# A hybrid decoder layer on one core: the last block of FFN down products computed with tokens on the partitions, the second layer norm taken along the rows

## The chip, the cores and the metric

One NeuronCore of a Trainium2 chip runs the whole layer as one program. The metric is device time of one execution in microseconds (us). The engines are named as in the profile: PE is TensorE (PEld its weight loads), DVE VectorE, ACT ScalarE, POOL GpSimd, SP SyncE, which here only issues DMAs.

## The reference, cut to what matters

The layer handles 1024 prompt tokens and 32 sample tokens (8 sequences of 4), 1056 in all, of 1024 features. After attention, the state space branch and a first norm, the part that matters is:

```python
def swiglu_ffn(h, w_ffn_gate, w_ffn_up, w_ffn_down):
    g = jnp.einsum('btd,df->btf', h, w_ffn_gate)
    u = jnp.einsum('btd,df->btf', h, w_ffn_up)
    return jnp.einsum('btf,fd->btd', jax.nn.silu(g) * u, w_ffn_down)
...
    h = layer_norm(ALPHA * x + mix, ln1_g, ln1_b)
    y = layer_norm(ALPHA * h + swiglu_ffn(h, w_ffn_gate, w_ffn_up, w_ffn_down), ln2_g, ln2_b)
```

`D_FF` is 2816, everything is float32. `y` (1056 x 1024) goes to HBM with one token per row.

## The kernel before

Activations stand transposed, features on the 128 partitions and the 1056 tokens along the free dimension: `mm[P, KT, TOK]` is the residual, KT = 8 feature tiles. Products of near float32 precision are made of three products of rounded halves (`whi`/`wlo` for weights, `ahi`/`alo` or `fhi`/`flo` for activations: hi·hi, hi·lo, lo·hi). SP loads each weight unit (128 x 1024) into `raw`; POOL splits it into `whi` (L771) and then `wlo` (L773) in one of two slots, and starts a unit only when PE is done with the one that had its slot (`unit_done`); `unit_split` tells PE that both halves are there.

The FFN runs over NF = 11 blocks of 256 hidden features. In each, gate and up products (`dense`) are followed by `down` of the block before: two weight units, in each four feature tiles, the tile of 1056 tokens in three PSUM banks; DVE adds every result into `mm` (L2674). The blocks of the loop leave the last block's down products over, and the stage after the loop does these together with the norm.

That stage (the ending) goes by thirds of CH = 352 tokens. PE's `last_down(c, e0, e1)` makes for third c and feature tile e one PSUM bank in six products of 352 columns (L1642). DVE's `last_down` adds the bank into `mm` (L2870) and keeps a running sum over the tiles in `srow` (L2875). `mean` multiplies `srow` by a matrix of ones (L1567), ACT writes the mean row (L2051), DVE subtracts it (`centre`, L2775), ACT squares (L2058), DVE adds the squares of the eight tiles (`add_squares`, L2782), PE sums them over the partitions (L1574), ACT takes the root (L2063), DVE the reciprocal (L2787), PE spreads it over the partitions (`spread`, L1582), ACT copies it to `rsrow` (L2068), DVE multiplies by it and the gain (`scale`, L2790) and ACT adds the bias (`biased`, L2113). Then `by_token(i)` turns each tile of 128 tokens by eight transposes (L1659), ACT and DVE each copy half of it into `ytok[i]` (L2118, L2886), and SP stores it (L754). There are nine such tiles, the last with the 32 sample tokens (NS). The order on each engine is the order in which the code is written; waits are on semaphores counted, and a table `taken` gives second names to old semaphores (`step` is DVE's own, which it awaits before it reads what its last instruction wrote).

Of the kernel before, what the change touches and what calls it, by code (L numbers as in the profile page):

```python
# [11 lines left out]
ALU = mybir.AluOpType  # L12
# [3 lines left out]
P = 128  # L16
# [81 lines left out]
TS = 88  # L98
# [49 lines left out]
def build(nc, a, o, stop=99, debug=None):  # L148
# [6 lines left out]
             "tok_turned": ("x_turned", 9), "g_hi": ("x_hi", 9), "g_split": ("x_split", 9),  # L155
             "affine_ready": ("keys_turned", 9), "scaled": ("keys_out", 9), "centred": ("crow_turned", 6),
# [12 lines left out]
             "part_done": ("pre_ready", 36), "part_read": ("cb_read", 36), "squares_added": ("bf_ready", 2), "left_read": ("bt_read", 36), "uk_turned": ("norm_rooted", 2), "uk_ready": ("norm_inverted", 2), "lat_ready": ("norm_row", 6),  # L169
             "qlat_ready": ("norm_read", 6), "right_read": ("prod_ready", 32)}  # L170
# [239 lines left out]
    for pp in range(2):  # L410
# [3 lines left out]
        if pp == 1:  # L414
# [25 lines left out]
    stat, inv = ar("stat", [P, TOK // TS]), ar("inv", [P, TOK // TS])  # L440
    part, gnorm = ar("part", [P, TOK]), [rsrow, ar("gnorm1", [P, TOK])]
    ar = Arena(low)
    fhi, flo = ar("fhi", [P, 4, TOK], F32R), ar("flo", [P, 4, TOK], F32R)
    sq4 = [sq2[:, 0], sq2[:, 1], srow[:, :], murow[:, :]]
# [3 lines left out]
    sqb = [yz[:, :, :].rearrange("p a n -> p (a n)")[:, 0:KT * CH].rearrange("p (e n) -> p e n", n=CH),  # L448
           Arena(low + 34048 + 9 * 4096)("sqb", [P, KT, CH])]
# [24 lines left out]
    def _(sp):  # L474
# [425 lines left out]
    def _(pe):  # L900
# [668 lines left out]
        def square_sums(c, n):  # L1569

            pe.wait_ge(sem("row_read"), k["row_read"].held())
            pe.wait_ge(sem("squares_added"), k["squares_added"].next())
            for t in range(CH // TS):
                last = pe.matmul(ps[0:TS, 7, CH + t:CH + t + 1], sqb[n][:, 0, t * TS:(t + 1) * TS], ones[:, 0:1], start=True, stop=True)  # L1574
            last.then_inc(sem("sums_done"), k["sums_done"].adds(1))
# [16 lines left out]
        square_sums(0, 0)  # L1592
# [3 lines left out]
        square_sums(1, 0)  # L1596
# [3 lines left out]
        square_sums(2, 0)  # L1600
# [28 lines left out]
        for b in range(2):  # L1629
            pe.wait_ge(sem(f"res_free{b}"), k[f"res_free{b}"].next())  # L1630

        def last_down(c, e0, e1):

            for e in range(e0, e1):
                if c == 0 and e % 4 == 0:
                    pe.wait_ge(sem("unit_split"), k["unit_split"].next())
                if c * KT + e >= 6:
                    pe.wait_ge(sem("part_read"), k["part_read"].next())
                for i in range(6):
                    j, part = divmod(i, 3)  # L1640
                    w, x = ((whi, fhi), (whi, flo), (wlo, fhi))[part]
                    last = pe.matmul(ps[:, (c * KT + e) % 6, 0:CH], w[e // 4][:, j * 512 + e % 4 * P:j * 512 + (e % 4 + 1) * P], x[:, j, third(c)],  # L1642
                                     start=i == 0, stop=i == 5)
                last.then_inc(sem("part_done"), k["part_done"].adds(1))

        thirds_scaled = [0]

        def by_token(i):
            n = P if i < 8 else NS
            if i == 0:  # L1650
                pe.wait_ge(sem("part_read"), k["part_read"].next(6))
            if i >= 3:
                pe.wait_ge(sem("left_read"), k["left_read"].next())
                pe.wait_ge(sem("right_read"), k["right_read"].next())
            while thirds_scaled[0] * CH < i * P + n:
                pe.wait_ge(sem("affine_ready"), k["affine_ready"].next(KT))
                thirds_scaled[0] += 1
            for e in range(KT):
                last = pe.transpose(ps[0:n, 2 * (i % 3) + e // 4, e % 4 * P:(e % 4 + 1) * P], mm[:, e, i * P:i * P + n], ident)  # L1659
            last.then_inc(sem("tok_turned"), k["tok_turned"].adds(1))  # L1660

        last_down(0, 0, 8)
        last_down(1, 0, 3)
        mean(0)
        last_down(1, 3, 8)
        last_down(2, 0, 2)
        mean(1)
        square_sums(0, 1)
        last_down(2, 2, 6)
        spread(0)  # L1670
        last_down(2, 6, 8)
        mean(2)
        square_sums(1, 1)
        by_token(0)
        by_token(1)
        spread(1)
        square_sums(2, 1)
        spread(2)
        for i in range(2, 9):
            by_token(i)  # L1680
# [4 lines left out]
    def _(act):  # L1685
# [367 lines left out]
        def squares(c, n):  # L2053
            for h in range(2):
# [3 lines left out]
                act.activation(sqb[n][:, 4 * h:4 * h + 4, :], mm[:, 4 * h:4 * h + 4, third(c)], ACT.Square).then_inc(sem("squared"), k["squared"].adds(1))  # L2058
# [17 lines left out]
        squares(0, 0)  # L2076
        mean_row(1)
        root_of(0)
        squares(1, 0)
# [4 lines left out]
        squares(2, 0)  # L2084
# [25 lines left out]
        def biased(c):  # L2110
            for e in range(KT):
                act.wait_ge(sem("scaled"), k["scaled"].next())
                act.activation(mm[:, e, third(c)], mm[:, e, third(c)], ACT.Identity, bias=vecs[:, V_L2B + e:V_L2B + e + 1]).then_inc(sem("affine_ready"), k["affine_ready"].adds(1))  # L2113

        def left_half(i):
            n = P if i < 8 else NS
            act.wait_ge(sem("tok_turned"), k["tok_turned"].next())
            act.activation(ytok[i][0:n, 0:512], ps[0:n, 2 * (i % 3), :], ACT.Copy).then_inc(sem("left_read"), k["left_read"].adds(1))  # L2118

        mean_row(0)  # L2120
        squares(0, 1)
        mean_row(1)
        root_of(0)
        squares(1, 1)
        factor_row(0)
        mean_row(2)
        biased(0)
        root_of(1)
        squares(2, 1)
        factor_row(1)  # L2130
        left_half(0)
        left_half(1)
        biased(1)
        root_of(2)
        factor_row(2)
        left_half(2)
        biased(2)
        for i in range(3, 9):
            left_half(i)
# [3 lines left out]
    def _(dve):  # L2143
# [633 lines left out]
        def add_squares(n):  # L2777

            for h in (4, 2, 1):
                dve.wait_ge(sem("squared") if h == 4 else step.sem, k["squared"].next(2) if h == 4 else step.same())  # L2780
                total = k["squares_added"] if h == 1 else step
                dve.tensor_tensor(sqb[n][:, 0:h, :], sqb[n][:, 0:h, :], sqb[n][:, h:2 * h, :], ALU.add).then_inc(total.sem, total.adds(1))  # L2782
# [24 lines left out]
        add_squares(0)  # L2807
# [3 lines left out]
        add_squares(0)  # L2811
# [5 lines left out]
        add_squares(0)  # L2817
# [47 lines left out]
        def last_down(c, e0, e1):  # L2865

            at = third(c)
            for e in range(e0, e1):
                dve.wait_ge(sem("part_done"), k["part_done"].next())
                dve.tensor_tensor(mm[:, e, at], ps[:, (c * KT + e) % 6, 0:CH], mm[:, e, at], ALU.add).then_inc(sem("part_read"), k["part_read"].adds(1))  # L2870
                if e:
                    dve.wait_ge(sem("part_read"), k["part_read"].same())
                    dve.wait_ge(step.sem, step.same())
                    total = k["srow_ready"] if e == KT - 1 else step
                    dve.tensor_tensor(srow[:, at], mm[:, 0, at] if e == 1 else srow[:, at], mm[:, e, at], ALU.add).then_inc(total.sem, total.adds(1))  # L2875

        def scale_third(c):
            dve.wait_ge(sem("row_read"), k["row_read"].next())
            dve.wait_ge(sem("centred"), k["centred"].same())
            for e in range(KT):  # L2880
                scale(e, V_L2G, c)

        def right_half(i):
            n = P if i < 8 else NS
            dve.wait_ge(sem("tok_turned"), k["tok_turned"].next())
            dve.tensor_copy(ytok[i][0:n, 512:1024], ps[0:n, 2 * (i % 3) + 1, :]).then_inc(sem("right_read"), k["right_read"].adds(1))  # L2886

        last_down(0, 0, 8)
        last_down(1, 0, 3)
        centre(0)  # L2890
        last_down(1, 3, 8)
        add_squares(1)
        last_down(2, 0, 2)
        centre(1)
        inverse(0)
        last_down(2, 2, 8)
        add_squares(1)
        scale_third(0)
        centre(2)
        inverse(1)  # L2900
        add_squares(1)
        right_half(0)
        right_half(1)
        scale_third(1)
        inverse(2)
        right_half(2)
        scale_third(2)
# [25 lines left out]
```

## Time and profile before

| | |
|---|---|
| median of 3 timed runs | 2940.25 us (2938.14 to 2943.52) |
| profiled execution, its own time | 2930.37 us |
| its span in the trace | 2928.3 us |
| busy: PE, PEld, DVE, ACT, POOL | 96%, 86%, 51%, 26%, 35% |
| mean granted TensorE clock | 0.978 of full speed |

The span is what the trace shows from the first to the last instruction; the profiled execution took 2.1 us more. Times below count from the start of the span. The granted clock is given in parts of full speed: 1.00 is 2.4 GHz and 0.50 is 1.2 GHz. Neighbouring matmuls overlap in the trace, so what one costs in a stream is the distance of the starts and not its duration.

### The profile page before, as it was taken

The numbers are of one execution on the slowest core, as the hardware profiler recorded it, in microseconds if no ns is written. First come the engines' busy times: TensorE is split into PE (matmuls) and PEld (weight loads), VectorE is DVE, ScalarE is ACT, GpSimd is POOL, SyncE is SP. The second block draws the span as 40 slices with busy tenths as digits, with TensorE's granted clock in tenths as the row PEclk, the third lists the DMA queues.
The fourth block names the chain that finished last, engine by engine and source line by source line (L and its number), as shares of the span: only waits on it lengthen the run. The fifth ranks groups of instructions, "written<-read, shape, count | busy, mean of one in ns | idle before, by whom it ended". The sixth has DMA issues, their size and how long they took to land.

```text
span 2928.3 us, 45789 instructions
## 1 busy us (share of the span) xinstructions
PE 2821.5 (96%) x18912; PEld 2529.6 (86%) x18912; DVE 1501.4 (51%) x2094; ACT 762.3 (26%) x1193; POOL 1015.2 (35%) x603
## 2 busy tenths in 40 slices
PE   8999999999999999999999799999899999999996
PEld 7999999899999984555666599999799999999995
DVE  3535777766665655555344457863732222222227
ACT  2112112444454534454332321100310000000004
POOL 3443333333333315444112033444143333333330
PEclk9999999999999988999999899999999999999998
DMA  4363233565656644222534243343111111111101
GB/s 142 83 205 100 81 110 107 168 168 163 173 156 167 155 143 111 60 59 66 198 136 191 90 142 125 133 149 108 37 44 51 43 43 50 43 43 44 49 21 60
DMA packets 314482, 308.68 MB, mean 105 GB/s; under 512 B 32069, under 2 KB 272970, under 8 KB 311850
## 3 DMA queue, kind: packets, MB, share of 16 engines
q1 hardware_dynamic: 252104, 194.97, 23.6%
q10 hardware_dynamic: 58650, 73.89, 7.4%
q0 software_dynamic: 3584, 37.75, 3.4%
q8 instruction: 108, 1.77, 0.2%
q14 instruction: 36, 0.29, 0.0%
HBM read 228.36 MB, written 78.20 MB: 105 GB/s over the span
## 4 chain that ended last, share of the span: by engine, by line
PE 79%; DVE 11%; ACT 4%; issue 3%; DMA 1%; POOL 1%; ACTq 0%; SPq 0%; DVEq 0%; POOLq 0%
PE ps L964 41%; PE ps L1145 12%; PE ps L1279 4%; DVE cv L2287 3%; PE ps L1303 2%; PE ps L1293 2%; PE ps L1437 2%; PE ps L1413 2%; PE ps L1393 2%; PE ps L1178 1%; PE ps L1182 1%; PE ps L1171 1%; DVE cv L2281 1%; DVE cv L2289 1%; PE ps L1224 1%
## 5 line engine op out<-in xcount | busy, mean ns | idle before, releaser
L771 POOL TENSOR_TENSOR whi<-raw,cst 128x1024 fp32r<-128x1024 f32 x160 | 312.5, 1953 | 1151.2 <-PE ps L964 946.7
L773 POOL TENSOR_TENSOR wlo<-raw,whi 128x1024 fp32r<-128x1024 f32 x160 | 432.0, 2700 | 12.6
L964 PE MATMUL ps<-ahi,whi 128*128 128x352 f32 x1728 | 375.7, 325 | 2.1 <-POOL wlo L773 1.4
L964 PE MATMUL ps<-alo,whi 128*128 128x352 f32 x1728 | 375.6, 325 | 0.0
L964 PE MATMUL ps<-ahi,wlo 128*128 128x352 f32 x1728 | 372.4, 324 | 0.0
L964 PEld LDWEIGHTS ps<-ahi,whi 128*128 128x128 f32 x1728 | 294.7, 189 | 2.7 <-POOL wlo L773 1.7
L964 PEld LDWEIGHTS ps<-ahi,wlo 128*128 128x128 f32 x1728 | 296.8, 189 | 0.0
L964 PEld LDWEIGHTS ps<-alo,whi 128*128 128x128 f32 x1728 | 295.4, 188 | 0.0
L1145 PE MATMUL ps<-xhi,whi 128*128 128x352 f32 x768 | 255.9, 333 | 0.5 <-ACT xraw L1775 0.5
L1145 PE MATMUL ps<-xhi,wlo 128*128 128x352 f32 x768 | 247.8, 323 | 0.0
L1145 PE MATMUL ps<-xlo,whi 128*128 128x352 f32 x768 | 247.7, 323 | 0.0
L877 POOL TENSOR_TENSOR pr<-pr,rowinv 128x384 f32<-128x384 f32 (+7 forms) x128 | 145.6, 1146 | 192.0 <-DVE rowinv L2493 191.8
L2488 DVE TENSOR_REDUCE negmax<-ps 128x1 f32<-128x384 f32 (+7 forms) x128 | 97.0, 758 | 140.0 <-PE ps L1281 139.3
L1279 PE MATMUL ps<-kb,qb 96*128 96x512 f32 (+3 forms) x384 | 161.3, 539 | 6.0 <-ACT pr L1903 2.7
L2674 DVE TENSOR_TENSOR mm<-ps,mm 128x1056 f32<-128x1056 f32 x80 | 100.6, 1257 | 116.3 <-PE ps L964 116.3
L964 PE MATMUL ps<-xhi,whi 128*128 128x352 f32 x672 | 147.9, 329 | 5.2 <-ACT xraw L1775 3.9
L1279 PEld LDWEIGHTS ps<-kb,qb 96*128 96x128 f32 x384 | 65.6, 198 | 100.3 <-issue 84.5
L1145 PEld LDWEIGHTS ps<-xhi,whi 128*128 128x128 f32 x768 | 144.3, 188 | 8.7 <-issue 6.2
L964 PE MATMUL ps<-xlo,whi 128*128 128x352 f32 x672 | 147.2, 327 | 0.0
L964 PE MATMUL ps<-xhi,wlo 128*128 128x352 f32 x672 | 145.9, 326 | 0.0
L1145 PEld LDWEIGHTS ps<-xlo,whi 128*128 128x128 f32 x768 | 144.4, 188 | 0.0
L1145 PEld LDWEIGHTS ps<-xhi,wlo 128*128 128x128 f32 x768 | 144.3, 188 | 0.0
(372 smaller groups left out, 5082.3 us busy)
## 6 DMA issues: line engine op xcount, KB each, us to landing
raw<-in_w_in SPq DMA_DIRECT2D x61, 512.0 KB, 5.0
s_a<-d_acum SPq DMA_DIRECT2D x32, 512.0 KB, 7.3
d_xbc<-so ACTq DMA_DIRECT2D x24, 528.0 KB, 2.7
gt<-d_g SPq DMA_DIRECT2D x24, 528.0 KB, 3.7
raw<-in_w_ffn_gate SPq DMA_DIRECT2D x22, 512.0 KB, 3.8
raw<-in_w_ffn_up SPq DMA_DIRECT2D x22, 512.0 KB, 3.7
raw<-in_w_ffn_down SPq DMA_DIRECT2D x22, 512.0 KB, 3.5
d_z<-zo ACTq DMA_DIRECT2D x16, 528.0 KB, 5.0
```

What stands on the lines that cost most here:

```text
L771: pool.tensor_tensor(whi[s][:, :], raw[:, u], ones[:, 0:1].broadcast_to([P, UNIT]), ALU.mult).then_inc(sem("unit_hi"), k["unit_hi"].adds(1))
L773: pool.tensor_tensor(wlo[s][:, :], raw[:, u], whi[s][:, :].bitcast(F32), ALU.subtract).then_inc(sem("unit_split"), k["unit_split"].adds(1))
L877: pool.tensor_tensor(pr[G][i][:, :], pr[G][i][:, :], rowinv[:, n:n + 1].broadcast_to([P, length]), ALU.mult).then_inc(sem("n_ready"), k["n ...
L964: last = pe.matmul(ps[0:m, 3 * b + c, 0:width], w(j), x[:, j, at:at + width], start=i == 0, stop=i == n - 1)
L1145: last = pe.matmul(ps[:, b, 0:CH], w[u % SPLIT][:, j * P:(j + 1) * P], x[:, j, c * CH:(c + 1) * CH], start=i == 0, stop=i == 3 * KT - 1)
L1279: pe.matmul(ps[:, first_bank + c // 512, 0:w], qb[pp][h][:, q * P:(q + 1) * P], kb[pp][h][:, c:c + w], start=True, stop=True)
L1293: last = pe.transpose(ps[:, 4 + h, c * P:(c + 1) * P], pr[G][2 * (3 - c) + h][:, kb_ * P:(kb_ + 1) * P], ident)
L1303: last = pe.matmul(ps[64 * h:64 * h + 64, 6 + G, c0 * P:512], vb[pp][h][:, kb_, :], ptb[kb_ % 2][h][:, c0 * P:512], start=first, stop=kb_ ...
L1393: last = pe.transpose(ps[:, 4 + i % 3, r * P:(r + 1) * P], src, ident)
L2287: dve.scalar_tensor_tensor(out=cv[b][:, 0:SEQ], in0=xraw[b][:, j:j + SEQ], scalar=tap(j), in1=cv[b][:, 0:SEQ], op0=ALU.mult, op1=ALU.add). ...
L2488: dve.tensor_reduce(negmax[:, n:n + 1], src, AX, ALU.max, negate=True).then_inc(sem("m_ready"), k["m_ready"].adds(1))
L2674: dve.tensor_tensor(thirds(mm[:, e]), out3(b), thirds(mm[:, e]), ALU.add).then_inc(sem(f"res_free{b}"), k[f"res_free{b}"].adds(1))
```

## The change

The last block's down products are made with the activations as the stationary operand: for tile i of 128 tokens, `fhi`/`flo` (128 hidden features x 128 tokens) are loaded as weights and the split weights stream through, 512 output features at a time. Twelve products of 512 columns fill two PSUM banks with tokens on the partitions and 1024 features along them. Into the same accumulation go eight float32 products with `mm[:, e, tokens]` stationary and the identity moving, which add the residual and all earlier blocks, turned, and close the group. Four pairs of banks, (6, 7), (0, 1), (2, 3), (4, 5), are used in turn; from the fifth tile on PE waits for DVE's `tile_read` of the tile four before.

The norm goes along the row: DVE takes `bn_stats` of each bank (mean and variance of 512), `bn_aggr` joins them, one instruction subtracts the mean and multiplies by the gain while it leaves PSUM, ACT takes the root of variance + eps, DVE inverts it, and a last instruction multiplies by it and adds the bias. SP loads gain and bias broadcast over the partitions (512 KB each) behind the last weights. Transposes, mean, square sums and spread at the end of the kernel are gone; for the first norm they stay, with one buffer `sqb` in place of two.

```diff
@@ sync
+        for row, name in ((gain, "ln2_g"), (offset, "ln2_b")):
+            sp.dma_start(row[:, :], a[name][0].partition_broadcast(P)).then_inc(sem("rows_full2"), k["rows_full2"].adds(16))
         for i in range(9):
             n = P if i < 8 else NS
-            sp.wait_ge(sem("left_read"), k["left_read"].next())
-            sp.wait_ge(sem("right_read"), k["right_read"].next())
+            sp.wait_ge(sem("tok_ready"), k["tok_ready"].next())
@@ tensor
         pe.wait_ge(sem("f_split"), k["f_split"].next(2))
-        for b in range(2):
-            pe.wait_ge(sem(f"res_free{b}"), k[f"res_free{b}"].next())
-
-        def last_down(c, e0, e1):
...
+        def last_down(i):
+
+            n = P if i < 8 else NS
+            at, bank = slice(i * P, i * P + n), (6, 0, 2, 4)[i % 4]
+            if i >= 4:
+                pe.wait_ge(sem("tile_read"), k["tile_read"].next())
+            for s in range(2):
+                if i == 0:
                     pe.wait_ge(sem("unit_split"), k["unit_split"].next())
+                for m in range(6):
+                    j, part = divmod(m, 3)
                     w, x = ((whi, fhi), (whi, flo), (wlo, fhi))[part]
+                    pe.matmul(ps[0:n, bank + s, :], x[:, j, at], w[s][:, j * 512:(j + 1) * 512], start=m == 0, stop=False)
             if i == 0:
+                for b in range(2):
+                    pe.wait_ge(sem(f"res_free{b}"), k[f"res_free{b}"].next())
             for e in range(KT):
+                last = pe.matmul(ps[0:n, bank + e // 4, e % 4 * P:(e % 4 + 1) * P], mm[:, e, at], ident, start=False, stop=e % 4 == 3)
+            last.then_inc(sem("tile_done"), k["tile_done"].adds(1))
+
+        for i in range(9):
+            last_down(i)
@@ scalar
+        for i in range(9):
             n = P if i < 8 else NS
+            act.wait_ge(sem("var_ready"), k["var_ready"].next())
+            act.activation(deviation[0:n, i:i + 1], moments[0:n, i, 1:2], ACT.Sqrt, bias=epsc[0:n, 1:2]).then_inc(sem("std_ready"), k["std_ready"].adds(1))
@@ vector
+        dve.wait_ge(sem("rows_full2"), k["rows_full2"].next(32))
+
+        def normed(i):
+
             n = P if i < 8 else NS
+            bank = (6, 0, 2, 4)[i % 4]
+            dve.wait_ge(sem("tile_done"), k["tile_done"].next())
+            for s in range(2):
+                dve.bn_stats(out=halves[0:n, i, s, :], in_=ps[0:n, bank + s, :]).then_inc(step.sem, step.adds(1))
+            dve.wait_ge(step.sem, step.same())
+            dve.bn_aggr(out=moments[0:n, i, :], in_=halves[0:n, i, :, :]).then_inc(sem("var_ready"), k["var_ready"].adds(1))
+            dve.wait_ge(sem("var_ready"), k["var_ready"].same())
+            dve.scalar_tensor_tensor(out=ytok[i][0:n, :], in0=ps[0:n, bank:bank + 2, :].rearrange("p a n -> p (a n)"), scalar=moments[0:n, i, 0:1],
+                                     in1=gain[0:n, :], op0=ALU.subtract, op1=ALU.mult).then_inc(sem("tile_read"), k["tile_read"].adds(1))
+            dve.wait_ge(sem("std_ready"), k["std_ready"].next())
+            dve.reciprocal(factor[0:n, i:i + 1], deviation[0:n, i:i + 1]).then_inc(sem("inv_done"), k["inv_done"].adds(1))
+            dve.wait_ge(sem("inv_done"), k["inv_done"].same())
+            dve.wait_ge(sem("tile_read"), k["tile_read"].same())
+            dve.scalar_tensor_tensor(out=ytok[i][0:n, :], in0=ytok[i][0:n, :], scalar=factor[0:n, i:i + 1], in1=offset[0:n, :],
+                                     op0=ALU.mult, op1=ALU.add).then_inc(sem("tok_ready"), k["tok_ready"].adds(1))
```

On PE, at the start of the ending, before the change (moving operand first, then the stationary one; `_50`/`_52` are the halves of the first unit, `_51`/`_53` those of the second; `key_turned`, `half_done` and `st_turned` are the registers behind `res_free1`, `res_free0` and `f_split`, `cb_read` that behind `part_read`):

```order
L1642 MATMUL ps<-fhi,whi_50 128x352 [waits key_turned,unit_split,half_done,st_turned]
L1642 MATMUL ps<-flo,whi_50 128x352
L1642 MATMUL ps<-fhi,wlo_52 128x352
...
L1642 MATMUL ps<-fhi,whi_51 128x352 [waits unit_split]
L1642 MATMUL ps<-flo,whi_51 128x352
L1642 MATMUL ps<-fhi,wlo_53 128x352
...
```

24 products stand between the first of these and the first that needs the second unit. After the change, the same place and on to the second tile:

```order
L1647 MATMUL ps<-whi_50,fhi 128x512 [waits unit_split,st_turned]
L1647 MATMUL ps<-whi_50,flo 128x512
L1647 MATMUL ps<-wlo_52,fhi 128x512
...
L1647 MATMUL ps<-whi_51,fhi 128x512 [waits unit_split]
L1647 MATMUL ps<-whi_51,flo 128x512
L1647 MATMUL ps<-wlo_53,fhi 128x512
...
L1652 MATMUL ps<-cst,mm 128x128 [waits key_turned,half_done]
L1652 MATMUL ps<-cst,mm 128x128 x7
```

Six products now stand before the second unit is needed, and the wait for DVE's last additions (`res_free0`, `res_free1`) has moved from the first product to the first identity product.

On DVE, near the end of the kernel, before the change (`x_turned` is behind `tok_turned`, `rows_ready` behind `rooted`):

```order
L2782 TENSOR_TENSOR sqb<-sqb 128x352 [waits dve_step]
L2886 COPY ytok_241<-ps 128x512 [waits x_turned]
L2886 COPY ytok_242<-ps 128x512 [waits x_turned]
L2790 SCALAR_TENSOR_TENSOR mm<-mm,vecs,rsrow 128x352 [waits crow_turned,u_exp]
L2790 SCALAR_TENSOR_TENSOR mm<-mm,vecs,rsrow 128x352 x7
L2787 RECIPROCAL inv<-stat 88x4 [waits rows_ready]
L2886 COPY ytok_243<-ps 128x512 [waits x_turned]
```

and after it, one tile, of which there are nine (`x_turned` is behind `tile_done`, `keys_turned` behind `var_ready`, `pre_ready` behind `std_ready`, `bt_read` behind `tile_read`, `cb_read` behind `inv_done`):

```order
L2823 BN_STATS halves<-ps 128x6 [waits x_turned]
L2823 BN_STATS halves<-ps 128x6
L2825 BN_AGGR moments<-halves 128x2 [waits dve_step]
L2827 SCALAR_TENSOR_TENSOR ytok_248<-ps,moments,gain 128x1024 [waits keys_turned]
L2830 RECIPROCAL factor<-deviation 128x1 [waits pre_ready]
L2833 SCALAR_TENSOR_TENSOR ytok_248<-ytok_248,factor,offset 128x1024 [waits bt_read,cb_read]
```

The chain from adding to scaling that spanned a third of the tokens is now six instructions in one tile, and the tile's only wait for PE is ahead of its first.

## Rows read from the trace of the kernel before

**Rows 1.** The page: the span and the engines' busy time

```profile
span 2928.3 us, 45789 instructions
PE 2821.5 (96%) x18912; PEld 2529.6 (86%) x18912; DVE 1501.4 (51%) x2094; ACT 762.3 (26%) x1193; POOL 1015.2 (35%) x603
```

**Rows 2.** Chain that ended last, from 2800 on: start, length, what

```profile
2905.57 4.06 ACT mm L2113 x8
...
2919.22 5.37 PE ps L1659 x32
...
2924.60 0.68 DVE ytok L2886
```

**Rows 3.** Busy time by stretch: PE, PEld, DVE, ACT, POOL, granted clock, DMA

```profile
2855.20:2873.30 18.10, 18.09 (x110) 17.65 (x110) 15.85 (x29) 3.23 (x3) 2.91 (x2) 1.00 0.01 1
2873.30:2925.30 52.00, 28.61 (x161) 26.11 (x160) 42.30 (x69) 26.78 (x46) 0.00 (x0) 0.74 0.17 69
2879.60:2883.00 3.40, 3.40 (x14) 3.40 (x14) 3.40 (x5) 1.80 (x3) 0.00 (x0) 0.50 0.00 0
```

**Rows 4.** Timeline of PE about the start of the ending

```profile
2853.02 0.64 PE L964 MATMUL ps<-fhi,wlo 128*128 128x352 f32 x3
2855.21 0.40 PE L1642 MATMUL ps<-fhi,whi 128*128 128x352 f32 x1 [1.55 <-DVE mm L2674]
```

**Rows 5.** Timeline of POOL there: the split of the last weight unit

```profile
2853.81 1.89 POOL L771 TENSOR_TENSOR whi<-raw,cst 128x1024 fp32r<-128x1024 f32 x1 [7.26 <-PE ps L964]
2855.78 2.41 POOL L773 TENSOR_TENSOR wlo<-raw,whi 128x1024 fp32r<-128x1024 f32 x1
```

**Rows 6.** Timeline of PE: products of 512 columns in a stream

```profile
181.29 0.63 PE L964 MATMUL ps<-kn_lo,whi 128*128 128x512 f32 x2
...
183.15 0.63 PE L964 MATMUL ps<-kn_hi,wlo 128*128 128x512 f32 x2
```

**Rows 7.** Timeline of PE: plain float32 products between split ones

```profile
1685.23 2.81 PE L1509 MATMUL ps<-cst,inv 88*128 88x88 f32 x24
1687.83 0.73 PE L964 MATMUL ps<-ahi,whi 128*128 128x352 f32 x3
1688.40 0.64 PE L964 MATMUL ps<-alo,whi 128*128 128x352 f32 x3
...
537.84 0.39 PE L1162 MATMUL ps<-s_c,s_b 128*128 128x128 f32 x2
...
538.22 0.32 PE L1145 MATMUL ps<-xlo,whi 128*128 128x352 f32 x1
```

**Rows 8.** Groups of DVE by line and shape: busy, mean ns, idle before

```profile
L2886 DVE COPY ytok<-ps 128x512 f32<-128x512 f32 x8 | 5.3, 686 | 6.1 <-PE ps L1659 6.1
L2488 DVE TENSOR_REDUCE negmax<-ps 128x1 f32<-128x1024 f32 x16 | 19.6, 1224 | 36.9 <-PE ps L1281 36.9
L2790 DVE SCALAR_TENSOR_TENSOR mm<-mm,vecs,rsrow 128x352 f32<-128x352 f32 x48 | 25.8, 577 | 2.1 <-ACT rsrow L2068 2.1
L2493 DVE RECIPROCAL rowinv<-rowsum 128x1 f32<-128x1 f32 x128 | 19.8, 154 | 1.7 <-ACT pr L1903 0.9
```

**Rows 9.** Timeline of DVE: two copies in a row

```profile
2903.77 1.28 DVE L2886 COPY ytok<-ps 128x512 f32<-128x512 f32 x2
```

**Rows 10.** Timeline of ACT: a mean row, the root's table, a root

```profile
2866.66 0.47 ACT L2051 ACTIVATE murow<-ps 128x352 f32<-128x352 f32 x1 [33.68 <-PE ps L1567]
...
2876.72 1.28 ACT L2063 ACT_TABLE_LOAD   x1
2879.80 0.26 ACT L2063 ACTIVATE stat<-ps,epsc 88x4 f32<-88x4 f32 x1 [1.79 <-PE ps L1574]
```

**Rows 11.** Timeline of SP's queue: last weights, last store

```profile
2776.95 35.06 SPq L489 DMA_DIRECT2D raw<-in_w_ffn_down  x4
...
2925.36 0.33 SPq L754 DMA_DIRECT2D out_y_sample<-ytok  x1
```

**Rows 12.** The page: DMA issues, KB each, us to landing

```profile
raw<-in_w_ffn_down SPq DMA_DIRECT2D x22, 512.0 KB, 3.5
```

More of the change, by code:

```diff
@@ L443, in build @@
     fhi, flo = ar("fhi", [P, 4, TOK], F32R), ar("flo", [P, 4, TOK], F32R)
+    ar = Arena(at_part)
+    gain, offset = ar("gain", [P, D_MODEL]), ar("offset", [P, D_MODEL])
+    moments, halves = ar("moments", [P, 9, 2]), ar("halves", [P, 9, 2, 6])
+    deviation, factor = ar("deviation", [P, 9]), ar("factor", [P, 9])
     sq4 = [sq2[:, 0], sq2[:, 1], srow[:, :], murow[:, :]]
@@ L1573, in square_sums @@
             for t in range(CH // TS):
-                last = pe.matmul(ps[0:TS, 7, CH + t:CH + t + 1], sqb[n][:, 0, t * TS:(t + 1) * TS], ones[:, 0:1], start=True, stop=True)
+                last = pe.matmul(ps[0:TS, 7, CH + t:CH + t + 1], sqb[:, 0, t * TS:(t + 1) * TS], ones[:, 0:1], start=True, stop=True)
             last.then_inc(sem("sums_done"), k["sums_done"].adds(1))
@@ L1591, in _ @@
         mean(1)
-        square_sums(0, 0)
+        square_sums(0)
         unit_third(7, 2)
@@ L1628, in _ @@
         pe.wait_ge(sem("f_split"), k["f_split"].next(2))
-        for b in range(2):
-            pe.wait_ge(sem(f"res_free{b}"), k[f"res_free{b}"].next())
-        def last_down(c, e0, e1):
-            for e in range(e0, e1):
-                if c == 0 and e % 4 == 0:
+        def last_down(i):
[5 more added lines that the diff above has]
+                if i == 0:
@@ L1636, in last_down @@
                     pe.wait_ge(sem("unit_split"), k["unit_split"].next())
[L1637 to L1640, printed above, removed]
+                for m in range(6):
+                    j, part = divmod(m, 3)
                     w, x = ((whi, fhi), (whi, flo), (wlo, fhi))[part]
-                    last = pe.matmul(ps[:, (c * KT + e) % 6, 0:CH], w[e // 4][:, j * 512 + e % 4 * P:j * 512 + (e % 4 + 1) * P], x[:, j, third(c)],
-                                     start=i == 0, stop=i == 5)
@@ L1644, in last_down @@
[L1644 to L1649, printed above, removed]
-            if i == 0:
[L1651 to L1657, printed above, removed]
-            for e in range(KT):
-                last = pe.transpose(ps[0:n, 2 * (i % 3) + e // 4, e % 4 * P:(e % 4 + 1) * P], mm[:, e, i * P:i * P + n], ident)
-            last.then_inc(sem("tok_turned"), k["tok_turned"].adds(1))
@@ L1662, in _ @@
[L1662 to L1680, printed above, removed]
+                    pe.matmul(ps[0:n, bank + s, :], x[:, j, at], w[s][:, j * 512:(j + 1) * 512], start=m == 0, stop=False)
@@ L2057, in squares @@
                     act.wait_ge(sem("sums_done"), k["sums_done"].same())
-                act.activation(sqb[n][:, 4 * h:4 * h + 4, :], mm[:, 4 * h:4 * h + 4, third(c)], ACT.Square).then_inc(sem("squared"), k["squared"].adds(1))
+                act.activation(sqb[:, 4 * h:4 * h + 4, :], mm[:, 4 * h:4 * h + 4, third(c)], ACT.Square).then_inc(sem("squared"), k["squared"].adds(1))
         def root_of(c):
@@ L2075, in _ @@
         mean_row(0)
-        squares(0, 0)
+        squares(0)
         mean_row(1)
         root_of(0)
-        squares(1, 0)
+        squares(1)
         factor_row(0)
@@ L2083, in _ @@
         root_of(1)
-        squares(2, 0)
+        squares(2)
         factor_row(1)
@@ L2108, in _ @@
                 k["res_free1"].n += 4
[L2110 to L2115, printed above, removed]
-            n = P if i < 8 else NS
[L2117 to L2139, printed above, removed]
+        for i in range(9):
+            n = P if i < 8 else NS
+            act.wait_ge(sem("var_ready"), k["var_ready"].next())
+            act.activation(deviation[0:n, i:i + 1], moments[0:n, i, 1:2], ACT.Sqrt, bias=epsc[0:n, 1:2]).then_inc(sem("std_ready"), k["std_ready"].adds(1))
     @block.vector
@@ L2781, in add_squares @@
                 total = k["squares_added"] if h == 1 else step
-                dve.tensor_tensor(sqb[n][:, 0:h, :], sqb[n][:, 0:h, :], sqb[n][:, h:2 * h, :], ALU.add).then_inc(total.sem, total.adds(1))
+                dve.tensor_tensor(sqb[:, 0:h, :], sqb[:, 0:h, :], sqb[:, h:2 * h, :], ALU.add).then_inc(total.sem, total.adds(1))
         def inverse(c):
@@ L2806, in _ @@
         last_residual(1)
-        add_squares(0)
+        add_squares()
         centre(1)
@@ L2810, in _ @@
         last_residual(2)
-        add_squares(0)
+        add_squares()
         for b in range(2):
@@ L2816, in _ @@
         inverse(1)
-        add_squares(0)
+        add_squares()
         split_third(1)
@@ L2863, in _ @@
             dve.wait_ge(sem(f"res_free{b}"), k[f"res_free{b}"].same())
[L2865 to L2883, printed above, removed]
-            n = P if i < 8 else NS
-            dve.wait_ge(sem("tok_turned"), k["tok_turned"].next())
-            dve.tensor_copy(ytok[i][0:n, 512:1024], ps[0:n, 2 * (i % 3) + 1, :]).then_inc(sem("right_read"), k["right_read"].adds(1))
-        last_down(0, 0, 8)
@@ L2889, in _ @@
[L2889 to L2907, printed above, removed]
-        for i in range(3, 9):
-            right_half(i)
+        dve.wait_ge(sem("rows_full2"), k["rows_full2"].next(32))
@@ L2911, in build @@
+        for i in range(9):
+            normed(i)
     ctx.close()
```

22 lines of the change are left out of this document (11 added, 11 removed).

## The prediction

> **What bounds the kernel now.** First the page: PE is busy for 96% of the span [rows 1], so nearly everywhere only PE's own work counts. The exception is the end. In the chain that ended last, read in order of time [rows 2], PE's products give way after 2873 to steps of DVE and ACT that follow one another over whole thirds. The busy time by stretch shows the same in two rows [rows 3]: from 2855.2 to 2873.3 PE works 18.09 of 18.10 us; from 2873.3 to 2925.3 it works 28.61 of 52.0 us, at a mean clock of 0.74, while DVE works 42.3. The change touches this stage and nothing ahead of it.
>
> I take the stage from the moment PE can issue the first product of the last block. PE's last product of the loop's `down` starts at 2853.02 + 2 x 0.16 = 2853.34 (the row holds three, 0.16 apart), so the next could start at 2853.5; it starts at 2855.21, since it waits for DVE's last addition [rows 4]. DVE's last copy ends at 2924.60 + 0.68 = 2925.28 [rows 2], and the span ends 3.0 us later, the store of the last tile, issued at 2925.36 [rows 11]. So the stage lasts 71.8 us, and 3.0 us of store follow. The change must be priced as a new stage from 2853.5.
>
> **The price of a tile on PE.** Twelve products of 512 columns: in a stream the first of eight starts at 181.29 and the one behind them at 183.15, 1.86 us for eight, 0.232 each [rows 6] (rows left out hold the other six), so 2.79 us. Eight identity products are plain float32. The trace shows that one such product is two instructions (L1162 x2 is one product). A pass of 128 columns with 128 weight columns costs 0.11: the first starts at 537.84, and the next product's own pace of 0.16 counted back from 538.22 gives 538.06, thus 0.22 for two. In a long run, 24 passes go from 1685.23 to 1687.83, 0.108 each, though they move only 88 columns [rows 7]. I take 0.112, 16 x 0.112 = 1.79 us; the bounds are 0.108 and, if loads and products overlap less when the moving side is longer, some 0.13 as an estimate (88 to 128 columns adding 0.02). Coming back from float32 to split products costs something: three products took 0.57 us in place of 0.48 [rows 7], 0.09. A tile is 2.79 + 1.79 + 0.09 = **4.67 us** (4.6 to 5.0). The ninth tile has 32 tokens, but the moving columns are the same, so I price it the same.
>
> A rule bears on the largest term. The Trainium skill (page "TensorE: Matmul & The Clock Gate", on the isolated single-matmul gap) gives about N/2.4 + 2.5 ns, 216 ns for 512 columns; the row shows 232. By it twelve products would take 2.59 us and nine tiles 1.8 us less than here; I go by the row, which has this kernel's own number format.
>
> **The start.** The first half of tile 0 needs only the first unit, which was split long ago, and banks 6 and 7, which the loop does not use: 2853.5 + 6 x 0.232 = 2854.9. The second half needs the last unit. POOL starts its split at 2853.81, when PE releases the slot, and ends it at 2855.78 + 2.41 = 2858.19 [rows 5]. Before, 24 products (3.9 us) covered that; now six do, and PE idles 3.3 us. This is the change's new wait, behind it stands everything on PE. The gain from moving the wait for DVE's addition (1.6 us [rows 4]) is therefore covered by this one and is worth nothing. Six products and 16 passes more: 2858.25 + 1.39 + 1.79 = 2861.4.
>
> **The clock after that wait.** From 2879.6 to 2883.0 PE ran full but at a clock of 0.50 [rows 3], after a stretch from 2873 on in which it mostly waited. Those 3.4 us did the work of 1.7. Whether the new pause of 3.3 us has the same effect the trace cannot settle: none of 0 to 1.7 us is excluded. The pause is nearer to the pause that cost than to the 1.55 us before 2855.2, after which the clock was 1.00 [rows 3, 4]. I take 1.4. The Trainium skill says the same of direction (same page, Part 1: the throttled clock is the default and only activity releases it); by that rule the full 1.7 would come due.
>
> **The end.** Tile 0 is ready at 2861.4 + 1.4 = 2862.8, tile 8 at 2862.8 + 8 x 4.67 = 2900.2, plus 0.2 for the last pass to drain (the last transpose likewise frees DVE only at its modelled end [rows 2]): 2900.4.
>
> **The price of a tile on DVE.** `bn_stats` is not in the trace. Its nearest rows read 512 float32 of PSUM in 0.69 us: the copy [rows 8], and a second one follows after 1.28 - 0.69 = 0.6 [rows 9]; a reduction of 1024 takes 1.22 [rows 8], so another element costs 1.05 ns whatever comes out. If an element costs this instruction twice that, it is about 1.2 us. I take 0.6 + 0.69; waiting for its own result costs 0.03. `bn_aggr` is tiny, like the reciprocal of one column, 0.154 [rows 8]: 0.16 + 0.03. The two large ones have 1024 elements and a scalar that is a column: L2790 with 352 takes 0.577; 672 more, at the 1.05 ns an element by which the copy of 512 and the reduction of 1024 differ, add 0.70, 1.28 each [rows 8]; the first overlaps its successor by some 0.08. The reciprocal again 0.19. Sum: 0.60 + 0.72 + 0.19 + 1.20 + 0.19 + 1.28 = **4.2 us**, below PE's 4.67: DVE waits in every tile and only its last one counts. ACT's root takes 0.26 and lies under the subtracting instruction; its table was loaded ahead of the wait before (2876.72, the root at 2879.80) [rows 10] and ACT has then been idle since 2833 (33.68 us before 2866.66), so no 1.28. The wait of PE for `tile_read` concerns a tile four back, some 14 us ago: free. Gain and bias, 1 MB, are issued behind the last weights at about 2812 [rows 11], 50 us before their use; if that cover went, they'd cost about two loads of 3.5 us [rows 12]. The stores are 512 KB each 4.7 us, longer apart than a transfer of that size takes [rows 12], so none queues.
>
> **Sum.** 2900.4 + 4.2 = 2904.6, + 3.0 of store = 2907.6 for the span of 2928.3: 20.7 us less. In the profiled execution's time 2930.37 becomes 2909.7; it lay 9.9 us below the median of the timed runs, so against these the time is 2940.25 - 20.7 = **2919.5 us**.
>
> **The rivals.**
> - *Forecast, PE bounds the stage* (0.75): 2919.5. With the clock staying up and 4.6 a tile it is 2 us less, 2917.5 (a little under with noise, 2915); with 5.0 a tile and the full 1.7 it is 3 us more, 2922.5.
> - *DVE bounds it* (0.15): `bn_stats` at twice the time an element. A tile is then 4.2 + 1.1 = 5.3 on DVE; it starts at 2862.9 and ends at 2862.9 + 9 x 5.3 = 2910.6, +3.0 = 2913.6, 14.7 us less: 2925.5. For it: an instruction that yields mean and variance does more per element than a copy. Against: the reduction pays nothing for its arithmetic [rows 8]. It decides above 4.67 a tile, that is from 0.24 us per `bn_stats` more.
> - *PE stays at half clock* (0.03), the case on the slower side: products of 512 columns at 0.43 and passes at 0.21 make a tile 8.5 us; 2858.25 + 5.9 + 8 x 8.5 + 4.2 + 3.0 = 2939.4, 11 us more: 2951. It decides from 7.1 us a tile. Against it: in [rows 3] from 2879.6 to 2883.0 the clock came back after 3.4 us of dense work, and the new stream has no waits in it.
> - *The gain is given back* (0.05): the long row stores or the broadcast loads hold up the end, or another layout of the program shifts the kernel before the stage by a few us; 2930 to 2940. Nothing in the trace speaks for it; the store of 128 KB at the end is the same one.
> - *Cheaper than thought* (0.02): passes of the identity at half the price (0.9 us less a tile) make DVE and PE even at 4.2 and save 4 us more: 2915.
>
> **How the numbers follow.** The measurement tells 0.2%, about 6 us, from no change. The range 2914 to 2926 holds the forecast with its bounds and run-to-run noise of 1 or 2 us, the cheaper case and most of the DVE case; outside stay the slower case, the given-back case and some noise, under 0.2. Faster 0.94, same 0.03, slower 0.03.
>
> **What the profile would show.** Right: an idle of about 3.3 us of PE ahead of the seventh product, released by POOL's L773 line; a PE stream with no gaps to the end, tile distance 4.7 us; DVE idle about 0.5 us in each tile, released by PE; the last DVE instruction about 4.2 us behind the last product. Wrong: `bn_stats` far over 0.7 us, PE waiting for `tile_read`, a clock of 0.50 for more than 4 us, or float32 passes far from 0.112.

## The result, and the profile after

The changed kernel takes 2921.47 us (median of six runs, 2916.29 to 2928.43) against 2942.82 us of six runs of the kernel before: a ratio of 0.9929 with a 95% interval of 0.9913 to 0.9946. That is 21.4 us less; 20.7 were forecast, and 2919.5 us for the time. The interval lies wholly below 1, so the gain is real; in microseconds it reaches from 16 to 26, so these medians cannot tell 20.7 from, say, 23.

The page of the changed kernel, its first lines as in [rows 1]:

```profile
span 2921.4 us, 45631 instructions
PE 2829.9 (97%) x18894; PEld 2533.1 (87%) x18894; DVE 1477.7 (51%) x2052; ACT 736.8 (25%) x1154; POOL 1015.3 (35%) x603
```

The two spans differ by 6.9 us only, and that is no measure of the change. The ending starts at 2868.8 in this execution and at 2853.5 in the profiled one of before: the untouched part ahead of it was 15 us longer here. The profiled execution of before was a short one: 2930.37 us, while none of its timed runs was under 2937. If the ending, the store and the 2.1 us outside the span are taken off the two medians, the ending starts at about 2866 before and 2867 now (an estimate from 2942.82 - 71.8 - 3.0 - 2.1 and 2921.47 - 50.3 - 2.3 - 1.8), so by this estimate the 15 us are no cost of the change. In the profiles of the eight kernels of this study, one execution each, the ending starts anywhere from 2853.5 to 2868.8. So the ending is compared by itself: from the first moment at which PE can issue a product of the last block to the end of DVE's last instruction. Before it lasted 71.8 us, by the prediction's reading of [rows 2, 4]; now it lasts 50.3, read as follows. First the timeline of PE at its start (start, length, engine, line, operation, and in brackets the idle time ahead and who ended it):

```profile
2868.79 0.39 PE L1647 MATMUL ps<-whi,fhi 128*128 128x512 f32 x1
...
2869.95 0.40 PE L1647 MATMUL ps<-wlo,fhi 128*128 128x512 f32 x1
2873.47 0.79 PE L1647 MATMUL ps<-whi,fhi 128*128 128x512 f32 x1 [3.12 <-POOL wlo L778]
2874.06 0.63 PE L1647 MATMUL ps<-whi,flo 128*128 128x512 f32 x1
```

Then the timeline of POOL, the split that ends that wait:

```profile
2869.10 1.90 POOL L776 TENSOR_TENSOR whi<-raw,cst 128x1024 fp32r<-128x1024 f32 x1 [7.24 <-PE ps L969]
2871.08 2.34 POOL L778 TENSOR_TENSOR wlo<-raw,whi 128x1024 fp32r<-128x1024 f32 x1
```

The first six products start at once, no longer held by DVE's last addition [rows 4]. The seventh waits 3.12 us for POOL, where the prediction had 3.3. Behind the wait the products start 0.43 us apart in place of 0.23, and in the same stretch the granted clock is half. Busy time by stretch, columns as in [rows 3]:

```profile
2873.50:2876.20 2.70, 2.70 (x7) 2.12 (x8) 0.00 (x0) 0.00 (x0) 0.00 (x0) 0.50 0.00 0
2878.00:2914.00 36.00, 36.00 (x220) 30.68 (x220) 32.66 (x48) 2.37 (x8) 0.00 (x0) 1.00 0.26 102
```

For 2.7 us the granted clock is 0.50, which is 1.2 GHz; from 2878 to 2914 PE works without a gap at 2.4 GHz. In the kernel before, the matching stretch had PE at 28.61 of 52.0 us [rows 3]. The whole ending in the same view, of the kernel before and then of the changed one:

```profile
2853.50:2925.30 71.80, 46.87 (x272) 43.78 (x270) 59.41 (x97) 30.01 (x49) 4.30 (x2) 0.81 0.13 50
2868.80:2919.10 50.30, 42.91 (x253) 36.13 (x252) 38.49 (x55) 2.66 (x9) 4.24 (x2) 0.95 0.21 84
```

PE's idle time fell from 24.9 to 7.4 us, and its busy time from 46.9 to 42.9; of the 21.5 us gained, 17.5 are idle time. The chain that ended last shows the tile's two parts and the tail, where before it changed from ACT to PE to DVE over whole thirds [rows 2]:

```profile
2905.62 2.78 PE ps L1647 x12
2908.40 1.78 PE ps L1652 x16
2910.19 2.78 PE ps L1647 x12
2912.97 1.88 PE ps L1652 x16
...
2914.87 1.29 DVE halves L2823 x2
...
2916.19 0.21 DVE moments L2825
...
2916.42 1.27 DVE ytok L2827
2917.69 0.08 DVE factor L2830
...
2917.80 1.27 DVE ytok L2833
```

A tile is 4.57 us of PE from start to start, and the last one is followed by 4.20 us of DVE, to 2919.07. The chain parts a tile at the ends of instructions, into 2.78 + 1.78 us; by the starts, as everywhere else here, it is 2.86 for the products and 1.70 for the sixteen float32 passes. The second tile in PE's timeline:

```profile
2877.98 0.48 PE L1647 MATMUL ps<-whi,fhi 128*128 128x512 f32 x1
2878.30 0.39 PE L1647 MATMUL ps<-whi,flo 128*128 128x512 f32 x1
...
2880.84 1.95 PE L1652 MATMUL ps<-cst,mm 128*128 128x128 f32 x16
2882.54 0.48 PE L1647 MATMUL ps<-whi,fhi 128*128 128x512 f32 x1
```

The first product behind the passes takes 0.32 us to the next start, the others 0.23. In every tile behind the first, DVE's chain begins with a short wait for PE, 0.22 to 0.39 us. The first DVE instruction of one tile, and the root's table and first root on ACT (timeline):

```profile
2905.66 1.29 DVE L2823 BATCH_NORM_STATS2 halves<-ps 128x6 f32<-128x512 f32 x2 [0.32 <-PE ps L1652]
...
2848.29 1.28 ACT L2089 ACT_TABLE_LOAD   x1
2879.93 0.29 ACT L2089 ACTIVATE deviation<-moments,epsc 128x1 f32<-128x1 f32 x1 [30.36 <-DVE moments L2825]
```

The table is loaded at 2848, long ahead of the first root at 2879.93. The span ends 2.3 us behind DVE's last instruction; before it was 3.0.

### The profile page after: what moved, and what is told of

It is laid out like the page before. It is cut to its first block, busy times and chain, and to the rows that moved or that the text cites. A ratio compares the mean times of both kernels' runs of the same rounds, so it can differ in the third digit from the quotient of the medians.

```text
span 2921.4 us, 45631 instructions
## 1 busy us (share of the span) xinstructions
PE 2829.9 (97%) x18894; PEld 2533.1 (87%) x18894; DVE 1477.7 (51%) x2052; ACT 736.8 (25%) x1154; POOL 1015.3 (35%) x603
## 4 chain that ended last, share of the span: by engine, by line
PE 81%; DVE 11%; ACT 3%; issue 3%; DMA 1%; POOL 1%; ACTq 0%; SPq 0%; POOLq 0%; DVEq 0%
PE ps L969 41%; PE ps L1150 12%; PE ps L1284 4%; DVE cv L2237 3%; PE ps L1308 2%; PE ps L1298 2%; PE ps L1442 2%; PE ps L1418 2%; PE ps L1398 2%; DVE cv L2231 1%; PE ps L1183 1%; PE ps L1187 1%; PE ps L1176 1%; PE ps L1647 1%; DVE cv L2239 1%
```

## The experiments

All lengths of "the ending" are read in the same way, from the first product of the last block to the end of DVE's last instruction. In that reading the changed kernel has 50.3 us. Device times are medians; the kernel before had 2943.75 us over ten runs beside them. The ending's length comes from one profiled execution of each kernel.

**First halves ahead.** PE issues the first unit's products for four tiles before it waits for the last unit. `half(i, s)` issues the six products of bank `s` of tile `i`, `turned(i)` its identity products (the two definitions are left out here).

```diff
...
+        pe.wait_ge(sem("unit_split"), k["unit_split"].next())
+        half(0, 0)
+        for b in range(2):
+            pe.wait_ge(sem(f"res_free{b}"), k[f"res_free{b}"].next())
+        for i in range(1, 4):
+            half(i, 0)
+        pe.wait_ge(sem("unit_split"), k["unit_split"].next())
+        for i in range(9):
+            if i >= 4:
+                pe.wait_ge(sem("tile_read"), k["tile_read"].next())
+                half(i, 0)
+            half(i, 1)
+            turned(i)
```

> Edit: the six products of the first weight unit are issued for tiles 0 to 3 before the wait for the last unit; nothing is left out. 'The ending' is the time from the first product of the last block to the end of the last VectorE instruction; the changed kernel has 50.3 us. Theory (TensorE bounds the ending, and the pause for POOL costs 3.1 us plus 1.2 us of half clock): with the pause filled the whole 4.3 us would come off if TensorE stayed the bound; but tiles 0 to 3 are then ready only 3.3 us apart, under VectorE's 4.25 us a tile, so VectorE takes over as the bound: tile 0 is ready about 9.1 us into the ending, nine tiles of 4.25 us follow, 47.3 us, 3.0 us less. Rival (the pause costs nothing, since VectorE or the stores set the end): 50.3 us, unchanged. Rival (TensorE stays the bound at 4.57 us a tile): 46.0 us. The device time against the changed kernel: 3 us less by the theory, which its run-to-run spread may hide; the trace decides.

Measured: 2916.61 us (five runs), ratio to before 0.9908 (0.9892 to 0.9923). The ending lasts 46.8 us, from 2864.49 to 2911.28. Busy time by stretch of this kernel:

```profile
2864.50:2869.00 4.50, 4.45 (x20) 3.34 (x20) 1.26 (x1) 0.00 (x0) 4.12 (x2) 1.00 0.01 4
2869.00:2873.00 4.00, 4.00 (x25) 3.48 (x24) 0.00 (x0) 0.00 (x0) 0.18 (x1) 1.00 0.00 0
2873.00:2906.00 33.00, 33.00 (x213) 28.30 (x211) 31.34 (x48) 2.36 (x8) 0.00 (x0) 1.00 0.28 112
```

PE has no pause, the clock is 1.00 in all three stretches, and 3.5 us came off, more than the half clock alone had cost (1.2): the pause was on the path. "Unchanged" falls. The device time is 4.9 us under that of the changed kernel, but the runs of the two overlap. The 46.0 of the rival in which PE stays the bound is 0.8 off, the 47.3 of the theory 0.5; DVE's timeline parts them, here the first instruction of tiles 0, 1 and 8:

```profile
2873.81 1.29 DVE L2829 BATCH_NORM_STATS2 halves<-ps 128x6 f32<-128x512 f32 x2 [7.87 <-PE ps L1647]
2877.98 1.29 DVE L2829 BATCH_NORM_STATS2 halves<-ps 128x6 f32<-128x512 f32 x2
...
2907.09 1.28 DVE L2829 BATCH_NORM_STATS2 halves<-ps 32x6 f32<-32x512 f32 x2
```

The tiles follow 4.16 us apart (33.28 for eight), with no wait for PE behind the first: DVE is the bound, as the theory had it.

**Two left banks ahead.** Tiles 0 and 1 get the products and the identity products of their left bank before the wait. `turned(i, s)` now makes the four identity products of one bank.

```diff
...
+        half(0, 0)
+        for b in range(2):
+            pe.wait_ge(sem(f"res_free{b}"), k[f"res_free{b}"].next())
+        turned(0, 0)
+        half(1, 0)
+        turned(1, 0)
+        pe.wait_ge(sem("unit_split"), k["unit_split"].next())
```

> Edit: before the wait for the last weight unit, tiles 0 and 1 get their first six products and the four identity products of their left bank; behind the wait only the right banks are left for these two tiles. Nothing is left out. Theory: this covers the 3.1 us pause (about 1.4 + 0.9 + 1.4 + 0.9 us of work), holds the clock, and has tile 0 ready 2.3 us behind POOL's split, about 7.1 us into the ending; then VectorE (9 x 4.25 us) and TensorE (tile 8 ready after 41.3 us, plus 4.2) end nearly together: 45.4 to 45.6 us for the ending against 50.3, 4.8 us less; against the kernel before some 26 us less, a ratio of about 0.991. Rival (the clock falls anyway): TensorE's products behind the wait take 0.43 us each for a while, 46.5 us or more. Rival (the pause was free): 50.3 us.

Measured: 2914.57 us (five runs), ratio 0.9906 (0.9891 to 0.9921), the lowest median of the study, though in device time not separable from "First halves ahead". The ending lasts 45.9 us (2862.27 to 2908.13). DVE's timeline in this kernel, the first instruction of tiles 0, 1, 6, 7 and 8:

```profile
2869.71 1.29 DVE L2834 BATCH_NORM_STATS2 halves<-ps 128x6 f32<-128x512 f32 x2 [5.98 <-PE ps L1647]
...
2873.87 1.29 DVE L2834 BATCH_NORM_STATS2 halves<-ps 128x6 f32<-128x512 f32 x2
...
2894.73 1.29 DVE L2834 BATCH_NORM_STATS2 halves<-ps 128x6 f32<-128x512 f32 x2
...
2899.29 1.29 DVE L2834 BATCH_NORM_STATS2 halves<-ps 128x6 f32<-128x512 f32 x2 [0.32 <-PE ps L1647]
2903.94 1.28 DVE L2834 BATCH_NORM_STATS2 halves<-ps 32x6 f32<-32x512 f32 x2 [0.40 <-PE ps L1647]
```

DVE starts tile 0 after 7.4 us in place of 9.6 and then goes 4.16 us a tile with no wait; its early tiles are behind PE, and only in the last two does it wait for PE again (0.32 and 0.40 us). The two engines end nearly together, as the theory had it (45.4 to 45.6 us), and the clock stays at 1.00: both rivals fall.

**The rows' norm alone.** The products and additions of before, then transposes, then the new norm.

```diff
...
+                last = pe.transpose(ps[0:n, 4 + 2 * (i % 2) + e // 4, e % 4 * P:(e % 4 + 1) * P], mm[:, e, i * P:i * P + n], ident)
...
+                dve.wait_ge(sem("part_done"), k["part_done"].next())
+                dve.tensor_tensor(mm[:, e, third(c)], ps[:, (c * KT + e) % 4, 0:CH], mm[:, e, third(c)], ALU.add).then_inc(sem("part_read"), k["part_read"].adds(1))
...
+        last_down(0, 0, 8)
+        last_down(1, 0, 4)
+        normed(0)
+        normed(1)
+        last_down(1, 4, 8)
+        last_down(2, 0, 4)
+        normed(2)
+        normed(3)
+        last_down(2, 4, 8)
+        for i in range(4, 9):
+            normed(i)
```

> Edit: only the norm along the rows is taken over. The last block's products stay as in the kernel before (features on the partitions, 352 tokens, VectorE adds each into the residual), then each tile of tokens is turned by eight transposes and normed along its row as in the changed kernel. Nothing is left out. Theory (most of the gain comes from taking the norm tile by tile along the row, which shortens VectorE's work and cuts the chain over whole thirds; the products' new layout mostly moves VectorE's additions to TensorE): VectorE has 24 additions of 0.45 us and nine tiles of 4.25 us, 49 us, and starts about 3 us into the ending: 52 us plus bubbles, 52 to 55 us against 50.3 of the changed kernel and 71.8 before. Rival (the gain comes from the products by token, which need no transposes and no additions on VectorE): well over 60 us.

Measured: 2930.79 us (five runs), ratio 0.9959 (0.9944 to 0.9973), by the medians 9.3 us slower than the changed kernel. The ending lasts 59.0 us from the first product and 60.7 with the wait for DVE ahead of it, which the 71.8 of before includes too. Both forecasts missed: the theory's 52 to 55 is 4 us short of the first reading and 6 of the second, and "well over 60" is not met either. DVE's groups in the ending of this kernel:

```profile
L2858 DVE TENSOR_TENSOR mm<-ps,mm 128x352 f32<-128x352 f32 x24 | 12.0, 521 | 9.1 <-PE ps L1652 9.1
L2842 DVE BATCH_NORM_STATS2 halves<-ps 128x6 f32<-128x512 f32 x16 | 10.3, 686 | 0.7 <-PE ps L1662 0.7
```

I had the 24 additions follow each other at 0.45 us. Sixteen of them wait for PE, 9.1 us in all, mostly because a bank's six products take 0.96 us. Two of the waits are longer, 1.1 us together, since PE had itself waited 4.2 us for DVE and then ran at a granted clock of 0.50 until 2887.6. In the order in which this kernel has the work, no norm runs in the place of these waits; another order was not tried. So the norm along the rows, in this order, is worth 71.8 - 60.7 = 11.1 us, and the step from there to the changed kernel, which rids DVE of the additions, the other 10.4: each about half, not most of it the norm's.

**No identity products.** They are left out, so the output lacks the residual and all earlier blocks; the last split product of each bank closes the group instead.

```diff
...
-            for e in range(KT):
-                last = pe.matmul(ps[0:n, bank + e // 4, e % 4 * P:(e % 4 + 1) * P], mm[:, e, at], ident, start=False, stop=e % 4 == 3)
```

> Edit: the eight identity products of each tile are left out, so the residual and all earlier blocks are missing from the output. Theory: a tile costs TensorE 2.8 us in place of 4.57, so VectorE becomes the bound at 4.25 us a tile: tile 0 is ready 7.4 us into the ending (with the pause and the half clock), nine tiles follow, 45.6 us against 50.3. The identity products thus cost 4.7 us of the ending though they hold TensorE for 16 us. Rival (VectorE or the stores are the bound already): 50 us, hardly less than now. Rival (TensorE alone sets the end): 9 x 1.8 = 16 us less, 34 us.

Measured: the ending lasts 45.2 us (one execution, 2918.16 us). The waits within it:

```profile
DVE halves L2821 <- PE ps L1647: 6.3, 1, 6.3
```

DVE waits for PE once, ahead of tile 0, and then never: DVE is the bound at 4.16 us a tile, as the theory had it (45.6); 50 and 34 us fall. The identity products hold PE for 16 us but cost the ending 5.1.

**The pause filled.** 13 products that are thrown away stand in the pause.

```diff
+                    for r in range(13 if s else 0):
+                        pe.matmul(ps[:, 7, :], fhi[:, 0, 0:P], whi[0][:, 0:512], start=True, stop=True)
```

> Edit: between the two halves of tile 0, ahead of the wait for the last weight unit, TensorE repeats one product of 512 columns 13 times into the bank that the second half then starts afresh; the result is the same and the wait ends at the same moment. Theory (the pause also costs half clock, 1.2 us): the six products behind the wait take 0.23 us each in place of 0.43, tile 0 is ready 1.2 us earlier relative to the first product, and the ending is 49.1 us against 50.3, with VectorE still waiting for TensorE in every tile. Rival (the slow products are the start-up of a stream after any wait, not the clock): 0.43 us again and 50.3 us.

Measured: the ending lasts 49.0 us (one execution, 2916.07 us). PE's timeline:

```profile
2864.18 3.20 PE L1644 MATMUL ps<-whi,fhi 128*128 128x512 f32 x13
2867.50 0.50 PE L1649 MATMUL ps<-whi,fhi 128*128 128x512 f32 x1
2867.84 0.39 PE L1649 MATMUL ps<-whi,flo 128*128 128x512 f32 x1
2868.07 0.40 PE L1649 MATMUL ps<-wlo,fhi 128*128 128x512 f32 x1
```

The products behind the wait start 0.23 us apart at a granted clock of 1.00, and 1.2 us come off, though nothing useful is done earlier. That agrees with the theory, but this one execution does not show that the filling kept the clock up: in the next experiment the same pause, not filled, was followed by full clock too. What does show that the 1.2 us were the clock is the two kinds of execution side by side: where the products behind the wait start 0.43 us apart the granted clock is 0.50, and where they start 0.23 apart behind an equal wait it is 1.00. The rival, slow products after any wait, falls by that.

**Row statistics twice.** DVE has 1.2 us more in each tile.

```diff
             for s in range(2):
+                dve.bn_stats(out=again[0:n, i, s, :], in_=ps[0:n, bank + s, :]).then_inc(step.sem, step.adds(1))
+            for s in range(2):
```

> Edit: VectorE takes the statistics of both banks twice, the first pair into a buffer that nobody reads. Theory (VectorE has only some 0.3 us of slack a tile under TensorE's 4.57 us): two more of 0.6 us make VectorE's tile 5.4 us, it becomes the bound, waits for TensorE only ahead of tile 0, and the ending is 9.6 + 9 x 5.4 = 58.2 us against 50.3, and TensorE waits for tile_read from about the eighth tile on or not at all. Rival (VectorE's work is covered and only the last tile's counts): 51.5 us.

Measured: the ending lasts 56.5 us (one execution, 2927.26 us). Two of the waits within it, and the busy time by stretch behind the pause:

```profile
DVE again L2824 <- PE ps L1653: 6.8, 1, 6.8
...
PE ps L1648 <- POOL wlo L779: 3.1, 1, 3.1
```

```profile
2871.20:2874.00 2.80, 2.71 (x17) 2.44 (x18) 0.00 (x0) 0.00 (x0) 0.04 (x1) 1.00 0.00 0
```

A tile on DVE is 5.36 us and DVE waits only ahead of tile 0; PE never waits for `tile_read`: 8.26 + 9 x 5.36 = 56.5. DVE's slack in the changed kernel is thus real but small, and the rival in which only its last tile counts falls. The expected 58.2 was 1.7 us too long, 1.3 of it for a reason of its own: here PE waited the same 3.1 us for POOL, and the clock stayed at 1.00. The same pause cost 1.2 us in the changed kernel and in the one without identity products (granted clock 0.50 from 2873.5 to 2876.2 in both), and nothing here. What decides between the two was not tried.

## Why the prediction was right, point by point

**What bounds the kernel.** Shown. Only the ending changed, and there PE's waits went: up to its last product PE is now idle for the 3.1 us of the pause, and then for DVE's last 4.2, in place of 24.9 in all. That PE sets the pace by a small margin only is shown by "No identity products" and "Row statistics twice": take from PE, or add to DVE, and DVE is the bound.

**A tile on PE, 4.67.** Measured 4.57. By the starts, the products with the change back from float32 take 2.86 (forecast 2.79 + 0.09), so these two terms were right. The sixteen passes take 1.70 us, 0.106 each, where I took 0.112 and had 0.108 as the lower bound: the bound read from the long run of passes [rows 7] was nearer than the choice. Eight tile distances make that 0.8 us. The Trainium skill (page "TensorE: Matmul & The Clock Gate", on the isolated single-matmul gap) has 216 ns for 512 columns at full clock; here the products start 0.23 us apart in every full-clock tile, so the trace does not follow it for this format, and going by the row was right.

**The start, 3.3 us of wait.** Measured 3.12. That it is on the path was shown by taking it away, with the half clock behind it: 3.5 us came off with the first halves ahead and 4.4 with the two left banks. The prediction's other half, that moving the wait for DVE's additions is worth nothing because this one stands behind it, was argued from rows and not tried: with the old wait of 1.6 us in place, PE's pause would have been in two parts, and what the clock does then no run shows.

**The clock, 1.4 us of 0 to 1.7.** Measured (0.43 - 0.23) x 6 = 1.2 in the changed kernel, the clock by the granted 0.50 in that stretch, and 0 in one execution of another kernel with the same pause. The full 1.7 came due in none. The range was right to keep down to 0: the price came in two executions of three. That the profiled one was among the two is luck for the 1.4.

**Tile 0 and tile 8.** Forecast 9.5 and 46.9 us behind the first product; DVE starts them after 9.57 and 46.08. The 0.8 us of the second is the tile's price above.

**A tile on DVE, 4.2.** Measured 4.20 at the end and 4.16 in a stream of tiles. Two `bn_stats` of 512 take 1.29, thus 0.60 and 0.69, as the nearest rows for reading PSUM gave; `bn_aggr` 0.21 (forecast 0.16); the large ones 1.28 each, as forecast. The rival with twice the time an element is refuted by its row. That DVE is nonetheless the next bound, 0.3 to 0.4 us under PE, was named as the point from which it decides (0.24 us more per `bn_stats`); twice the statistics went past it. PE's wait for `tile_read` was free, as forecast: DVE gave the first tile's banks free at 2881.2 and PE came to them at 2891.7, 10.5 us later.

**The store, 3.0 us.** This term was mis-sized: it is 2.3. The issues by size and time to landing in us, of the kernel before and then of the changed one, both from 2900 on:

```profile
out_y_sample<-ytok SPq DMA_DIRECT2D x1, 128.0 KB, 2.5
```

```profile
out_y_sample<-ytok SPq DMA_DIRECT2D x1, 128.0 KB, 1.9
```

Before, five stores of 512 KB were issued between 2919.6 and 2924.2; the last of them landed at 2927.5, after the 128 KB store had been issued at 2925.36, and that landed 0.4 us behind it. Now each store has 4.57 us to itself, the last large one has landed at 2917.1, two us ahead of the small one's issue, and the small one lands 0.6 us sooner. It also takes 1.9 us in "First halves ahead" and "The rows' norm alone", where the stores stand as far apart. I had noted that none would queue, and had not drawn that from the term.

**The sum.** Forecast 20.7 us; the ending gave 71.8 - 50.3 = 21.5 and the store 0.7 by the traces, 22.2 in all. The traces thus put the forecast 1.5 us too low, 0.8 by the passes' price and 0.7 by the store. The medians say 21.4, but with an interval from 16 to 26 us; that they came within 0.7 us of the forecast is partly luck. The slower cases did not come about: the clock came back within 2.7 us of work, and the loads of gain and bias were issued at 2827.4 and 2827.9, some 50 us ahead of their first use. That the part ahead of the ending did not grow with the change is the estimate given with the result (2866 and 2867), not a direct measurement.

## What to carry to other kernels

When the end of a kernel runs back and forth between engines over large pieces, work in the layout in which the last reduction goes along the free dimension, tile by tile, so that PE streams and one engine follows a tile behind; here the norm along the rows was worth about half of the gain, and the products by token, which took the additions off the follower, the other half. Count what covered a producer's last delivery before you reorder its consumer: six products in place of 24 uncovered 3.1 us, and issuing first what does not need the delivery covered all of it. After such a repair look at the engine next in line: it had only 0.3 to 0.4 us a tile of slack, so it took over as soon as PE's tiles came closer.

## What was not expected of the hardware

- One product of plain float32 with 128 stationary and 128 moving columns is two passes, 0.106 us each by the starts (16 in 1.70 us), and in the ninth tile, with 32 stationary columns, 16 passes take 1.93 us from the first start to the last end against 1.95 with 128: the narrower stationary operand bought nothing.
- The same pause of 3.1 us on PE was followed by half clock in two executions and by full clock in a third, each of another kernel.
- The start of the ending moved by up to 15 us between the eight profiled executions, though the kernels do the same work ahead of it, but for the two loads of gain and bias issued some 40 us before. Why is not known. Part of it is the clock: from 1390 to 1480 the mean granted clock is 0.96 in the kernel before and 0.92 in the changed one.
